# Three blocks of a language model on one core: the first unit of four layers works on x times the norm's weights, and the root comes in behind it

## Chip, core and metric

One core of one Trainium2 chip runs the whole program in one launch. The metric is the device time in microseconds. Every number of the trace is from one profiled execution.

## What is computed

x is 256 x 1024 in float32, and every weight is float32 in HBM (217 MB are read once). Two layers (pooling with spatial gating; gated linear attention with stick-breaking attention), then a block of feed-forward, a mixer (short convolution and an S5 state space), and a second feed-forward. Ahead of each stands the same thing: a norm, a scale and a shift that depend on the condition (columns of `ada`).

```python
def rms_norm(x, gain):
    return x * lax.rsqrt(jnp.mean(x * x, -1, keepdims=True) + EPS) * gain
mod = silu(cond) @ w_mod + b_mod                      # nine vectors of 1024; likewise ada_w for the first two layers
h = rms_norm(x, ffn1_norm) * (1 + sc1) + sh1
x = x + 0.5 * g1 * ((silu(h @ w_gate) * (h @ w_up)) @ w_down)
h = rms_norm(x, mix_norm) * (1 + sc2) + sh2
b_gate, c_gate, v, u = split(h @ w_in)                # 512 columns each
y_conv = b_gate * conv3(c_gate * v)
y_ssm = s5(u); y_ssm = y_ssm * sigmoid(y_ssm @ glu_w + glu_b)
x = x + g2 * (concat(rms_norm(y_conv), rms_norm(y_ssm)) @ w_out)
```

For a column of the weights W, h @ W is r (x G) @ W + sh @ W, with r the reciprocal root of the token, G = gain (1 + scale) per channel, and sh the shift.

## The kernel before

**Form of the data.** x is kept transposed in `xT`, eight tiles of 128 channels x 256 tokens. Each fp32 product is done as three fp32r products: high times high, high times low, low times high. ACT makes a high part by a copy that rounds (`WH` of weights, `hh` of h, `YH` of outputs), DVE makes the low part by a difference (`WL`, `hl`, `YL`).

**Units and pieces.** The weights are cut into units of 1 MB, each of two pieces of 128 x 1024. SP loads them in the order of `unit_list` (L106) into a ring of ten pieces. `cut` on ACT (L1176) makes WH up to three pieces ahead, `cut` on DVE (L1652) WL up to two ahead; four of each are kept, so WL of a piece also waits until PE is through with the piece four back. `cols_T` (L622) is a unit of 256 output columns, output transposed: eight k tiles with 6 products of 256 columns each. `wide` (L634) has hh and hl as the stationary side and 512 weight columns moving, and is used for the FFN's gate and up columns together. `out_rows` (L678) adds 256 rows of the output weights into `pacc`, 48 products; the last of a layer goes by quarters, so that `update` (L1763) on DVE can add each quarter to xT while PE does the next.

**ada.** The scales and shifts come from further units that only DVE works on: each half unit is one multiply and add of 128 x 1024 into `ACC` (L1675), the sums over the partitions are done by PE, and an "add" on DVE (L1681) stores eight columns. `weave` (L125) spreads these units among the others; `ada_places` (L191) says at which unit DVE does them, with a place "tail" behind the last unit of a layer.

**The seam between two layers.** Behind the last `out_rows`: ACT squares the eight tiles of the new xT, PE sums them over the channels (`stats`, L661), DVE computes the root in eight short dependent instructions (`newton`, L1717 to L1726), PE spreads it over the partitions (`spread`, L671), and `modulate` makes for each k tile on DVE xT times GS times root (L1755), on ACT the shift and high part hh, on DVE the low part hl (L1760). The first product of the next layer needs tile 0 of these. `norm_mod` (L731) and, ahead of FFN 1, the lines L1045 to L1051 put products on constants (`warm`) between. At FFN 1 two statistics are taken with weights `FG2`, as the first model's final norm stands in between; half of these sums stand between the quarters of the last out_rows. DVE's columns GS are made behind the update (`mod_cols`, L1740).

**Side work.** Preparation for S5 in FFN 1 and in MIX is written as generators; `side.run` takes `rate` steps of them per piece on each engine. PE's transposes ct (L981, L988) are such steps, with 6 idle ones ahead. PSUM has four banks for units, given in turn by `open_` and `back`. In MIX the order on PE is u, u, c, v, b, c, v, b, with the S5 steps in, out and turn (transposes back, L1098) between, then glu, which needs Y_G0 and Y_G1 (gelu of both halves of the S5 output; `gelu`, L2302), and the conv statistics.

**GpSimd** issues the S5 parameter loads (L2441, L2443) behind the last unit of the odd layer, masks the attention weights (L2402), and does little else.

## Time and profile before

| | us |
|---|---|
| median of 3 runs (lowest, highest) | 985.44 (983.79, 986.64) |
| the profiled execution | 985.16 |
| its span in the trace | 983.4 |
| PE busy | 951.5 |
| DVE busy | 713.7 |
| ACT busy | 508.8 |
| POOL busy | 40.9 |

Times in the rows are from the start of the span. The span is 1.8 us shorter than the execution's own time; what is compared with other runs is the latter. Busy times overlap; a row of a timeline ends with the idle time of its engine just ahead of it and with what ended that.

### The profile page before, as it was taken

What the parts mean: (1) busy time and instruction counts of PE and PEld (TensorE: products, weight loads), DVE (VectorE), ACT (ScalarE), POOL (GpSimd) and SP (SyncE); (2) the same over time, 40 slices, a digit from 0 to 9 for tenths busy, and PEclk for the clock granted to TensorE, in tenths of its full rate; (3) what the DMA queues carried; (4) which work ended last, traced back from release to release, by engine and by line L of the source; (5) the groups of instructions that cost most, each with busy time, mean ns of one, the idle gap of its engine ahead of it and who ended that gap; (6) DMA issues with size and microseconds to landing.
All of it is one profiled execution on the core that took longest, in us unless ns stands there. A gap on an engine that the chain in (4) does not pass through costs nothing.

```text
span 983.4 us, 17238 instructions
## 1 busy us (share of the span) xinstructions
PE 951.5 (97%) x7025; PEld 875.3 (89%) x7025; DVE 713.7 (73%) x994; ACT 508.8 (52%) x745; POOL 40.9 (4%) x68
## 2 busy tenths in 40 slices
PE   6999999999999999999999999999999999999998
PEld 5799989989899889999778889889998978898987
DVE  4778877767957946675998988967888765555554
ACT  4654364446645555644755456475555554444444
POOL 2100000000000013210100000000000000000000
PEclk9999999999999999999999999999999999999999
DMA  9998676846875877576577887774534457676631
GB/s 365 385 342 257 211 268 231 283 129 226 291 259 167 295 261 250 179 260 213 155 254 255 281 274 263 246 257 136 172 119 138 131 172 247 184 223 212 192 101 43
DMA packets 134247, 219.43 MB, mean 223 GB/s; under 512 B 8585, under 2 KB 100090, under 8 KB 134168
## 3 DMA queue, kind: packets, MB, share of 16 engines
q1 hardware_dynamic: 132416, 214.99, 66.3%
q0 software_dynamic: 992, 1.76, 0.7%
q10 hardware_dynamic: 760, 1.59, 0.4%
q8 instruction: 55, 0.90, 0.4%
q14 instruction: 24, 0.20, 0.1%
HBM read 217.25 MB, written 1.05 MB: 222 GB/s over the span
## 4 chain that ended last, share of the span: by engine, by line
PE 88%; DVE 7%; DMA 2%; issue 2%; ACT 1%; ACTq 0%; DVEq 0%
PE pw L568 62%; PE pacc L568 24%; DVE WL L1659 1%; DMA ring<-in_ada_w 1%; DVE SQT L1755 1%; DVE hl L1760 1%; PE pw L1021 1%; DMA cst<-in_consts 1%; DVE ACC L1675 1%; ACT hh L1174 1%; DVE AR L1675 0%; PE pw L997 0%; DVE xT L2059 0%; ACT WH L1174 0%; ACT SQT L1174 0%
## 5 line engine op out<-in xcount | busy, mean ns | idle before, releaser
L1174 ACT ACTIVATE WH<-ring 128x1024 fp32r<-128x1024 f32 x288 | 302.7, 1057 | 271.1 <-PE pw L568 171.7
L1659 DVE TENSOR_TENSOR WL<-ring,WH 128x1024 fp32r<-128x1024 f32 x288 | 348.3, 1224 | 84.2 <-ACT WH L1174 83.5
L568 PE MATMUL pacc<-YH,WH 128*128 128x256 f32 x672 | 192.8, 287 | 2.7 <-issue 1.7
L568 PE MATMUL pacc<-YH,WL 128*128 128x256 f32 x672 | 190.1, 283 | 0.0
L568 PE MATMUL pacc<-YL,WH 128*128 128x256 f32 x672 | 190.0, 283 | 0.0
L568 PE MATMUL pw<-hh,WH 128*128 128x256 f32 x704 | 186.7, 287 | 1.5 <-DVE WL L1659 0.8
L568 PE MATMUL pw<-hh,WL 128*128 128x256 f32 x704 | 183.9, 283 | 0.0
L568 PE MATMUL pw<-WH,hh 128*128 128x512 f32 x448 | 177.3, 396 | 2.8 <-DVE WL L1659 2.3
L568 PE MATMUL pw<-WL,hh 128*128 128x512 f32 x448 | 175.2, 391 | 0.0
L568 PE MATMUL pw<-hl,WH 128*128 128x256 f32 x704 | 142.6, 284 | 0.0
L568 PEld LDWEIGHTS pw<-hh,WH 128*128 128x128 f32 x704 | 134.8, 191 | 6.0 <-issue 5.7
L1174 ACT ACTIVATE AR<-pw 128x512 f32<-128x512 f32 (+8 forms) x180 | 80.3, 467 | 113.8 <-PE pw L568 110.5
L568 PE MATMUL pw<-WH,hl 128*128 128x512 f32 x448 | 138.4, 390 | 0.0
L568 PEld LDWEIGHTS pw<-hh,WL 128*128 128x128 f32 x704 | 135.0, 192 | 0.0
L568 PEld LDWEIGHTS pacc<-YH,WH 128*128 128x128 f32 x672 | 128.7, 192 | 5.4 <-issue 3.0
L568 PEld LDWEIGHTS pacc<-YL,WH 128*128 128x128 f32 x672 | 128.8, 192 | 0.7
L568 PEld LDWEIGHTS pacc<-YH,WL 128*128 128x128 f32 x672 | 128.7, 192 | 0.0
L1675 DVE SCALAR_TENSOR_TENSOR ACC<-ring,PC,ACC 128x1024 f32<-128x1024 f32 x95 | 121.7, 1281 | 2.4 <-DMA ring<-in_ada_w 2.2
L568 PEld LDWEIGHTS pw<-hl,WH 128*128 128x128 f32 x704 | 109.5, 192 | 0.1
L568 PEld LDWEIGHTS pw<-WH,hh 128*128 128x128 f32 x448 | 84.5, 189 | 23.2 <-DVE WL L1659 3.6
L568 PEld LDWEIGHTS pw<-WH,hl 128*128 128x128 f32 x448 | 84.4, 188 | 18.0
L568 PEld LDWEIGHTS pw<-WL,hh 128*128 128x128 f32 x448 | 84.5, 189 | 16.4
(272 smaller groups left out, 778.2 us busy)
## 6 DMA issues: line engine op xcount, KB each, us to landing
ring<-in_w_mod SPq DMA_DIRECT2D x72, 512.0 KB, 4.7
ring<-in_odd_in_w SPq DMA_DIRECT2D x56, 512.0 KB, 5.8
ring<-in_ada_w SPq DMA_DIRECT2D x48, 512.0 KB, 6.9
ring<-in_ffn_w_gate SPq DMA_DIRECT2D x88, 256.0 KB, 3.3
ring<-in_ffn_w_up SPq DMA_DIRECT2D x88, 256.0 KB, 4.3
ring<-in_ffn_w_down SPq DMA_DIRECT2D x44, 512.0 KB, 4.6
ring<-in_even_in_w SPq DMA_DIRECT2D x40, 512.0 KB, 6.5
ring<-in_even_out_w SPq DMA_DIRECT2D x16, 512.0 KB, 5.6
```

What stands on the lines that cost most here:

```text
L568: return eng.matmul(o, a, b, start=start, stop=stop, skip_group_check=True)
L1021: last = eng.transpose(pb[:, n * T + m * P:n * T + m * P + P], fbuf(blk, m)[:, n * P:n * P + P], ident)
L1174: return eng.activation(dst, src, func, **kw)
L1659: tt(WL[:, i % NL, :], slot(half_of(i)), WH[:, i % NH, :].bitcast(F32), SUB).then_inc(s_lo, 1)
L1675: stt(out=acc, in0=slot(g), scalar=wc, in1=acc, op0=MUL, op1=ADD).then_inc(s_ada, 1)
L1755: stt(out=SQT[:, k, :], in0=xT[:, k, :], scalar=GS[:, k:k + 1], in1=rb, op0=MUL, op1=MUL).then_inc(s_u, 1)
L1760: stt(out=hl[:, q, :], in0=SQT[:, q, :], scalar=m[:, q:q + 1], in1=hh[:, q, :].bitcast(F32), op0=ADD, op1=SUB).then_inc(s_hl, 1)
```

## The change

At the seams ahead of the odd layer, FFN 1, MIX and FFN 2 the first unit (qk0, gate and up columns of block 0, c, likewise) no longer waits for the root. ACT makes hh as the high part of xT times GS per tile (`early`), GpSimd makes xT times GS again and its low part hl (`lows`), and PE runs the first unit on these (`first`), with two more columns that hold the shift, so that their result is sh @ W. Half of the statistics come ahead of tile 0, half behind it, the spreading of the root ahead of tile 4. ACT copies both halves of the raw result (`RAW`) and the spread root (`RB`) to SBUF, GpSimd multiplies them (`rooted`), and ACT adds the shift's part (`biased`, or inside the Silu). From the second unit on the modulated tiles are used as before; DVE makes them with WL cuts between. The fillers at the seams go, GS is made ahead of the update, and the ada sums and adds go from the tails and the first two units (`QUIET`) to other units. In both FFNs gate and up columns of block 0 become two units in `cols` form, and the four transposes of that block go. The low-rank gate's 24 products go among the k tiles of qk1 and behind it, one output gate unit of the odd layer goes ahead of `at`. MIX begins with c, and the S5 steps keep their distances to the u units, with one unit fewer ahead of glu. The S5 parameter loads are issued after oo1 instead of oo7.

The diff, cut to its core:

```diff
-    def weave(side, from_, clear=0):
...
         k = 0
         for i, u in enumerate(main):
-            while k < len(side) and (2 * k + 1) * (len(main) - clear) <= 2 * i * len(side):
...
     def ffn(tag, Wg, Wu, Wd):
         for b in range(12):
-            if b < 11:
+            if b == 0:
...
+                cols(f"{tag}u0", Wu, 0)
+            elif b < 11:
...
-    weave(ada(a0, 2, 3) + ada(a1, 0, 2), at, 3)
+    weave(ada(a0, 2, 3) + ada(a1, 0, 2), at, 4)
...
-    weave(ada(a1, 2, 3) + ada(a2, 0, 4), at, 3)
+    weave(ada(a1, 2, 3) + ada(a2, 0, 4), at, 3, 2)
...
-    weave(ada(a2, 4, 8), at, 3)
-    for name, c0 in (("wu0", 1536), ("wu1", 1792), ("wc0", 512), ("wv0", 1024), ("wb0", 0), ("wc1", 768),
+    weave(ada(a2, 4, 8), at, 4, 2)
+    for name, c0 in (("wc0", 512), ("wu0", 1536), ("wu1", 1792), ("wv0", 1024), ("wb0", 0), ("wc1", 768),
                      ("wv1", 1280), ("wb1", 256)):
...
-    weave(ada(a2, 8, 9), at)
+    weave(ada(a2, 8, 9), at, 4, 2)
...
+        elif nm not in quiet:
             unit = nm
             add(nm)
-            if summed and summed[0][1]:
+            if summed and summed[0][1] and behind[nm] not in quiet:
                 total(nm)
...
-            if nm in tails:
-                key = "tail " + nm
-                total(key)
-                add(key)
+    assert not added and not summed
...
+FIRST = [None, "qk0", "f1g0", "wc0", "f2g0"]
+QUIET = ("eo7", "qk0", "qk1", "oo7", "f1g0", "f1u0", "f1d10", "wc0", "wu0", "wo3", "f2g0", "f2u0", "f2d10")
...
                         w = ones[:, 0:64] if weights is None else weights[:, k, :].unsqueeze(2).to_broadcast([P, 2, 32])
                         stats(st["pb"][:, 0:256], w, k, SQ_FIN[L] + k, k == 0, k == 7)
+                def rest():
+                    sums(2)
+                    sums(3)
+                    full[f"fin{L}"] = (s_sqr, sqr_n[0])
...
+                later[L] = rest
...
-                    if weights is not None and q >= 2 and h == 0:
-                        sums(q - 2)
                     if q == 3 and h == 1:
-                        if weights is None:
-                            sums(0)
-                            sums(1)
-                        sums(2)
-                        sums(3)
-                        full[f"fin{L}"] = (s_sqr, sqr_n[0])
+                        sums(0)
+                        sums(1)
+                        if L == L_F2:
+                            rest()
                 return tail
-            def norm_mod(L, z):
-                ada("tail " + TAIL[L - 1])
-                back(f"fin{L - 1}")
-                if L >= L_MIX:
-                    warm(5, f"warm{L}a")
-                spread(f"r{L}", 0, z, (s_u, 8 * L + 8), True)
-                warm(4, f"warm{L}b")
+            later = {}
+            def first(L, z, c=0):
+                name = FIRST[L]
+                k, a = unit(name)
+                names = first_banks(L)
+                bks = [open_(nm, None, True) for nm in names]
+                for half in range(2):
+                    H, Lo = piece(2 * k + half, a)
+                    for kk in range(4):
+                        i = 4 * half + kk
+                        if i == 1:
+                            later[L - 1]()
+                            back(f"fin{L - 1}")
+                        if i == 4:
+                            spread(f"r{L}", c, z, (s_rb, L), True)
+                        p.wait_ge(s_eh, 8 * (L - 1) + i + 1)
+                        for m, pb in enumerate(bks):
+                            mm(pb[:, 0:T + 2], H[:, kk, m * P:m * P + P], hh[:, i, 0:T + 2], i == 0, False)
+                            mm(pb[:, 0:T + 2], Lo[:, kk, m * P:m * P + P], hh[:, i, 0:T + 2], False, False)
+                        p.wait_ge(s_el, 8 * (L - 1) + i + 1)
+                        for m, pb in enumerate(bks):
+                            last = mm(pb[:, 0:T + 2], H[:, kk, m * P:m * P + P], hl[:, i, 0:T + 2], False, i == 7)
+                    last.then_inc(s_use, 1)
+                for nm in names:
+                    full[nm] = used(name)
+                    back(nm)
                 back(f"r{L}")
...
-            norm_mod(L_ODD, 2)
...
-            cols_T(L_ODD, "qk0")
...
-            for k in range(8):
-                last = mm3(pb[0:16, 0:T], (GRH[:, k, :], GRL[:, k, :]), hpair(L_ODD, k), k == 0, k == 7)
+            first(L_ODD, 2)
...
+            def low_rank(k):
+                if k == 0:
+                    open_("gl")
+                    p.wait_ge(s_grl, 1)
+                return mm3(pw[place["gl"]][0:16, 0:T], (GRH[:, k, :], GRL[:, k, :]), hpair(L_ODD, k), k == 0, k == 7)
+            cols_T(L_ODD, "qk1", None, lambda k: low_rank(k - 3) if k > 2 else None)
+            for k in range(4, 8):
+                last = low_rank(k)
...
-            cols_T(L_ODD, "qk1")
+            cols_T(L_ODD, "qk2")
...
+            gates = iter(range(8))
+            cols_T(L_ODD, f"og{next(gates)}")
...
-                yield from idle(6)
+                yield from idle(10)
...
+                    if blk == 0:
+                        cols_T(L, f"{tag}u0")
+                        if L == L_F1:
+                            spread("xnew", 8, 4)
+                            side.rate = 1
...
+            first(L_F1, 4, 10)
...
+            first(L_MIX, 5)
             for j in range(2):
                 cols_T(L_MIX, f"wu{j}", [(s_ura, j + 1), (s_urd, j + 1)])
             s5_in(0)
-            cols_T(L_MIX, "wc0")
+            cols_T(L_MIX, "wv0")
             s5_in(1)
-            cols_T(L_MIX, "wv0")
+            cols_T(L_MIX, "wb0")
             s5_out(0)
-            cols_T(L_MIX, "wb0")
+            cols_T(L_MIX, "wc1")
             s5_turn(0)
-            cols_T(L_MIX, "wc1")
+            cols_T(L_MIX, "wv1")
             s5_out(1)
-            cols_T(L_MIX, "wv1")
+            cols_T(L_MIX, "wb1")
             s5_turn(1)
-            cols_T(L_MIX, "wb1")
...
+            def early(L, sh, c, scale=1.0):
+                s.wait_ge(s_gs, L + 1)
+                s.wait_ge(*gone[f"ada{c}"])
+                s.wait_ge(*used(LAST_H[L]))
+                act(hh[:, :, T:T + 2], shift_cols(sh)).then_inc(s_esh, 1)
+                for q in range(4):
+                    ns = (2 * q, 2 * q + 1)
+                    if q == 3:
+                        squares(L - 1, ns)
+                        cut_on(L - 1)
+                    for n in ns:
+                        s.wait_ge(s_x, X_FIN[L - 1] + n + 1)
+                        act(hh[:, n, 0:T], xT[:, n, :], scale=GS[:, n:n + 1]).then_inc(s_eh, 1)
+                    if q < 3:
+                        squares(L - 1, ns)
+                k = unit(FIRST[L])
+                cut(2 * k)
+                modulate(L, sh, range(4))
+                for m, nm in enumerate(first_banks(L)):
+                    s.wait_ge(*full[nm])
+                    act(RAW[L][:, m, :], pw[place[nm]][:, 0:T + 2], scale=scale).then_inc(s_bank[place[nm]], 1)
+                cut(2 * k + 1)
+                modulate(L, sh, range(4, 8))
+                act(RB[L], pw[place[f"r{L}"]][:, 0:T]).then_inc(s_rb, 1)
+            def biased(L, dsts, func=ACT.Identity):
+                for m, dst in enumerate(dsts):
+                    s.wait_ge(s_em, 2 * (L - 1) + m + 1)
+                    act(dst, dst, func, bias=RAW[L][:, m, T:T + 1]).then_inc(s_eu, 1)
...
+                pieces(f"{tag}u0")
+                if tag == "f1":
+                    evac("xnew", XNW, src=pw[place["xnew"]][:, 0:T])
+                    side.rate = 1
+                for m in range(2):
+                    s.wait_ge(s_em, 2 * (L - 1) + m + 1)
+                    act(fbuf(0, m), fbuf(0, m), ACT.Silu, bias=RAW[L][:, m, T:T + 1]).then_inc(s_sl, 1)
...
+            win("wb1", lambda: s5_rows(1))
+            yhigh(Y_G0, f2(YS[:, 0:2, :]), (s_gelu, 2))
             conv_squares(0)
+            gelu(1, 0)
+            conv_squares(1)
...
+            def between(L, g, sh, root):
+                update(L - 1, g)
+                k = unit(FIRST[L])
+                root()
+                cut(2 * k)
+                mods[0] += 1
+                modulate(L, sh, range(3))
+                cut(2 * k + 1)
+                modulate(L, sh, range(3, 8))
...
+            def lows(L, sh):
+                g.wait_ge(s_esh, L)
+                g.wait_ge(s_gs, L + 1)
+                eng.tensor_tensor(hl[:, :, T:T + 2], shift_cols(sh), hh[:, :, T:T + 2].bitcast(F32), SUB)
+                for k in range(8):
+                    xg = XG[L][:, k % 2, :]
+                    g.wait_ge(s_x, X_FIN[L - 1] + k + 1)
+                    eng.tensor_scalar(xg, xT[:, k, :], GS[:, k:k + 1], None, MUL).then_inc(s_eg, 1)
+                    g.wait_ge(s_eh, 8 * (L - 1) + k + 1)
+                    g.wait_ge(s_eg, 8 * (L - 1) + k + 1)
+                    eng.tensor_tensor(hl[:, k, 0:T], xg, hh[:, k, 0:T].bitcast(F32), SUB).then_inc(s_el, 1)
+            def rooted(L, dsts):
+                g.wait_ge(s_rb, L)
+                for m, nm in enumerate(first_banks(L)):
+                    g.wait_ge(*gone[nm])
+                    eng.tensor_tensor(dsts[m], RAW[L][:, m, 0:T], RB[L], MUL).then_inc(s_em, 1)
```

## Rows read from the trace of the kernel before

**Rows 1.** The page of the kernel before, its part 1
```profile
PE 951.5 (97%) x7025; PEld 875.3 (89%) x7025; DVE 713.7 (73%) x994; ACT 508.8 (52%) x745; POOL 40.9 (4%) x68
```

**Rows 2.** The chain that ended last, in order of time (start us, us, what)
```profile
192.92 17.46 PE pacc L568 x144
...
216.24 59.40 PE pw L568 x408
...
464.56 0.92 PE pacc L568 x6
...
667.14 8.63 PE pacc L568 x72
...
760.71 17.27 PE pacc L568 x144
777.98 2.04 PE pw L568 x64
...
831.11 10.91 PE pw L568 x48
...
861.99 0.44 PE pw L1021 x4
```

**Rows 3.** Timeline of PE at the seams (start, us, instruction, idle before)
```profile
461.48 0.73 PE L568 MATMUL pw<-RS,SQT 128*64 128x64 f32 x12 [0.41 <-ACT SQT L1174]
...
478.38 0.50 PE L568 MATMUL pw<-WH,hh 128*128 128x512 f32 x1 [0.78 <-DVE WL L1659]
...
688.62 0.36 PE L568 MATMUL pw<-hh,WH 128*128 128x256 f32 x1 [0.75 <-DVE WL L1659]
...
790.72 0.50 PE L568 MATMUL pw<-WH,hh 128*128 128x512 f32 x1 [1.26 <-DVE WL L1659]
```

**Rows 4.** Timeline of DVE at the seam into FFN 2
```profile
774.56 1.65 DVE L1769 SCALAR_TENSOR_TENSOR xT<-pacc,MOD,xT 128x256 f32<-128x256 f32 x4
...
781.56 0.16 DVE L1726 SCALAR_TENSOR_TENSOR RS<-RS 128x2 f32<-128x2 f32 x1
...
783.65 0.48 DVE L1760 SCALAR_TENSOR_TENSOR hl<-SQT,MOD,hh 128x256 fp32r<-128x256 f32 x1 [0.18 <-ACT hh L1174]
...
789.45 4.62 DVE L1659 TENSOR_TENSOR WL<-ring,WH 128x1024 fp32r<-128x1024 f32 x4
```

**Rows 5.** Groups of ACT by form: busy us, mean ns of one
```profile
L1174 ACT ACTIVATE SQT<-xT 128x256 f32<-128x256 f32 x40 | 15.8, 416 | 18.4 <-DVE xT L1769 18.4
```

**Rows 6.** Groups of POOL by form: busy us, mean ns of one
```profile
L2402 POOL TENSOR_SCALAR_AFFINE_SELECT AR<-AR 128x512 f32<-128x512 f32 x2 | 1.2, 635 | 36.8 <-ACT AR L1174 36.8
...
L2402 POOL TENSOR_SCALAR_AFFINE_SELECT AR<-AR 128x1024 f32<-128x1024 f32 x1 | 1.1, 1085 | 21.0 <-ACT AR L1174 21.0
```

**Rows 7.** Timelines of DVE and POOL in stick-breaking attention
```profile
371.37 1.30 DVE L1659 TENSOR_TENSOR WL<-ring,WH 128x1024 fp32r<-128x1024 f32 x1
...
382.45 2.44 DVE L1659 TENSOR_TENSOR WL<-ring,WH 128x1024 fp32r<-128x1024 f32 x2
...
382.60 2.44 POOL L2402 TENSOR_SCALAR_AFFINE_SELECT AR<-AR 128x128 f32<-128x128 f32 x2 [1.04 <-DVE AR L2012]
```

**Rows 8.** Timelines of DVE and PE in the pool unit
```profile
133.00 2.67 DVE L1675 SCALAR_TENSOR_TENSOR ACC<-ring,PC,ACC 128x1024 f32<-128x1024 f32 x2
...
136.37 0.36 PE L568 MATMUL pw<-YH,WH 128*128 128x256 f32 x1 [1.77 <-issue]
```

**Rows 9.** Timeline of PE in FFN 1
```profile
507.93 1.12 PE L988 MATMUL pw<-cst,AR 128*128 128x128 f32 x4 [2.31 <-DVE YL L1705]
```

**Rows 10.** Windows: busy us of PE, PEld, DVE, ACT, POOL, granted clock, DMA share, GB/s
```profile
508.00:512.00 4.00, 4.00 (x14) 3.34 (x15) 3.93 (x6) 0.76 (x2) 0.00 (x0) 0.61 0.90 296
```

**Rows 11.** Timelines of PE, ACT and DVE at the end of MIX
```profile
747.80 0.35 PE L568 MATMUL pw<-YH,WH 128*128 128x256 f32 x1 [0.46 <-DVE YL L1705]
...
741.50 1.11 ACT L1174 ACTIVATE AR<-pw 128x256 f32<-128x256 f32 x2
...
746.97 0.68 DVE L1705 TENSOR_TENSOR YL<-AR,YH 128x512 fp32r<-128x512 f32 x1
```

More of the change, by code:

```diff
@@ L129, in weave @@
         for i, u in enumerate(main):
-            while k < len(side) and (2 * k + 1) * (len(main) - clear) <= 2 * i * len(side):
+            while k < len(side) and (2 * k + 1) * (len(main) - clear - lead) <= 2 * (i - lead) * len(side):
                 units.append(side[k])
@@ L218, in ada_places @@
     m, unit = 0, None
+    names = [u[0] for u in units if u[0] != "ada"] + [None]
+    behind = dict(zip(names, names[1:]))
     for nm, *_ in units:
@@ L490, in build @@
         XNW = ar(512 * 3, T)
+        EW = [0, 16384, 8192, 19464, 8192]
+        RB = [ar(o, T) for o in EW]
+        XG = [v3(ar(o + T, 2 * T), 2) for o in EW]
+        RAW = [v3(ar(o + T, 2 * T + 4), 2) for o in EW]
         def fbuf(blk, m):
@@ L630, in cols_T @@
                                     (half == 0 and kk == 0, False), half == 1 and kk == 3)
+                        if behind is not None and (half, kk) != (1, 3):
+                            behind(4 * half + kk)
                     last.then_inc(s_use, 1)
@@ L1038, in ffn @@
                                  finish(L) if blk == 11 else None, (lambda: turn(blk)) if blk < 11 else None)
-            def xnew_back():
-                yield from idle(3)
-                back("xnew")
-                yield
-            ada("tail oo7")
-            back("fin1")
-            warm(6, "warm2a")
-            spread("r2", 10, 4, (s_u, 24), True)
-            spread("xnew", 8, 4, None, True)
-            warm(5, "warm2b")
-            back("r2")
-            side.gens.append(xnew_back())
-            side.rate = 1
+            side.rate = 0
             side.gens.append(s5_weights())
+            first(L_F1, 4, 10)
             ffn(L_F1, "f1", Y_F1)
             side.flush()
-            norm_mod(L_MIX, 5)
             def s5_in(h):
@@ L1358, in _, with gate @@
             eng.preload_act_table_set("silu_and_others")
+            def gate(j):
+                pieces(f"og{j}")
+                evac(f"og{j}", f2(GT[:, 2 * j:2 * j + 2, :]), func=ACT.Silu)
+            gate(0)
             s.wait_ge(s_kqe, 3)
@@ L1515, in ffn @@
                         if blk == 1:
-                            yhigh(y0, pw[place[f"{tag}t0"]][:, :], full[f"{tag}t0"])
+                            yhigh(y0, ar(0, 2 * T), gone[f"{tag}u0"])
                         pieces(f"{tag}u{blk}")
@@ L1915, in _ @@
                 pieces(f"eo{j}")
+            mod_cols(3, M1, "norm_g", 8)
             v.wait_ge(*gone["ada2"])
-            update(L_EVEN, M0[:, 16:24])
-            norm(L_EVEN)
-            ada("tail eo7")
-            mod_cols(3, M1, "norm_g", 8)
-            modulate(L_ODD, M1[:, 0:8])
+            between(L_ODD, M0[:, 16:24], M1[:, 0:8], lambda: norm(L_EVEN))
             def decay():
@@ L1966, in _ @@
             gates = iter(range(8))
+            pieces(f"og{next(gates)}")
             v.wait_ge(s_kqe, 3)
@@ L2002, in _ @@
                     b.then_inc(s_yf, 1)
-                pieces(f"og{next(gates)}")
+                if q == 0:
+                    pieces(f"og{next(gates)}")
             for j in range(4):
@@ L2181, in ffn @@
             def ffn(tag, y0, n0):
-                for blk in range(12):
+                pieces(f"{tag}u0")
+                if tag == "f1":
+                    side.rate = 1
+                b = place[f"{tag}u0"]
+                for m in range(2):
+                    v.wait_ge(*full[f"{tag}u0"])
+                    v.wait_ge(s_sl, n0 + m + 1)
+                    a = tt(fbuf(0, m), fbuf(0, m), pw[b][:, m * T:m * T + T], MUL)
+                a.then_inc(s_bank[b], 1)
+                for blk in range(1, 12):
                     if blk < 11:
@@ L2199, in half_gate @@
                 v.wait_ge(*v.step(ts(HG, m, 0.5, None, MUL)))
-            side.rate = 1
+            side.rate = 0
             side.gens += [update_x(), s5_coefs(), s5_weights(), s5_tables(), s5_kernel(), s5_skip()]
             ffn("f1", Y_F1, 0)
+            side.flush()
             half_gate(8, M2[:, 16:24])
-            update(L_F1, HG)
-            side.flush()
             mod_cols(9, M2[:, 24:48], "mix_norm")
-            norm(L_F1)
-            ada("tail f1d10")
-            modulate(L_MIX, M2[:, 24:32])
+            between(L_MIX, HG, M2[:, 24:32], lambda: norm(L_F1))
             def conv(j):
```

200 lines of the change are left out of this document (98 added, 102 removed).

## Prediction

> **What bounds the kernel now.** I read the page first: PE is busy 97% of 983.4 us, DVE 73%, ACT 52%, POOL 4% [rows 1]. So only PE time counts: what it has to do, and where it waits. The chain in order of time gives PE's own pace: 144 products of 256 columns in 17.27 us (0.12 each), 48 of 512 columns in 10.91 (0.227 each), the 64 of the norm's statistics in 2.04, four transposes in 0.44 [rows 2]. At that pace a unit of 48 x 256 takes 5.76 us. Then PE's timeline shows where it stands still. There are four seams, where one layer's output ends and the next layer needs its norm. Call E the end of the last product into pacc: 210.38, 465.48, 675.77 and 777.98 [rows 2]. At FFN 2 DVE has the root at 781.72 and makes the first hl at 783.65, E + 5.7 [rows 4]; of the time to there 2.04 are statistics, and the fillers behind them are no work. The second unit waits again, 1.26 us, for a low part of weights (WL) [rows 3], because DVE makes all the modulated tiles first and the WLs only from 789.45 [rows 4]. I take the start of the third unit as the yardstick: 790.72 + 5.46 = E + 18.2 here, 688.62 + 5.76 = E + 18.6 at MIX, 478.38 + 5.46 = E + 18.4 at FFN 1 [rows 3], and at the odd layer 216.24 + 6.3 + 2.9 + 5.8 (DVE-paced qk0, low-rank gate, qk1) = E + 20.9 [rows 2].
>
> **The seam after the change, without port trouble (FFN 2, times from E).** DVE updates x at the same times plus 0.2 for the columns now made ahead of it. ACT now does 16 instructions of 0.416 us [rows 5] there instead of 8 (a product with GS and a square per tile), so the last square is done at 2.9 instead of 1.6, the statistics at 3.3 instead of 2.0, the root at 5.0 instead of 3.7. PE does tile 0 ahead of the second half of the statistics, tiles 1 to 3 while the root is computed, spread (0.45), tiles 4 to 7: each tile is 6 products, 0.72, and the unit ends at 8.8. DVE goes on from the root with one WL (1.15 each by the four in 4.62 us [rows 4]), three modulated tiles (two instructions each, 0.8: there are 14 from 783.65 to 789.45 [rows 4]), the next WL at 9.2 to 10.3, five tiles. ACT puts the two RAW copies and a WH cut between its fourth and fifth hh, so the last hl is at 16.2, not 15. The second unit so ends at 16.6 instead of 14.5, and the third waits for its WL until 17.4. **Gain 0.8**, and 0.44 more because block 0 is born transposed; the narrow products (96 x 0.12 instead of 48 x 0.227, 0.6 dearer) are in the 17.4. So the seam's hole is filled, but DVE, already the pacer, takes most of it back. The same working gives 17.6 at MIX (gain 1.0), 19.0 at the odd layer with the low-rank products filling the waits (gain 1.9). FFN 1 loses today a wait of 0.41 in the tail, twice [rows 3], and 1.0 of statistics stand ahead of E there, which puts its comparable E 1.9 earlier: 18.4 + 1.9 - 17.9 = 2.4, and 0.44. Sum of the seams: -7.0. The two extra columns cost 1 in 128 of 5.76, under 0.05 per seam. The longer table load at the odd layer falls into ACT's wait ahead of the tail.
>
> **GpSimd.** It gets eight pairs per seam, a product (one input) and a difference (two inputs), then two products with the root. Its only comparable rows are masks: 0.635 us for 512 elements, 1.085 for 1024 [rows 6], so 0.88 ns per element and 0.185 fixed; 256 elements with one input 0.41, with two between 0.41 (the second input free) and 0.64 (twice the reading), taken near the upper end. A pair is then some 1.15 us, the eighth is ready at E + 6.6, PE wants it at 8.6: covered, up to 1.4 us a pair. At 2.0 a pair each seam would lose about 4.5.
> The Trainium skill (GPSIMD Engine Reference, 3.1) states 2.6 cycles per element for two inputs; as an estimate from that page the difference would take 0.7 us and the sum stays as it is.
>
> **The port.** While POOL masks 128 elements next to DVE's WLs, each mask takes as long as a WL (2.44 for two, beside two WLs in 2.44) instead of the 0.3 that the two rows above give for 128 elements, and the WLs are stretched by under 0.1 (1.30 for one [rows 7]; four undisturbed in 4.62 [rows 4]): the two engines exclude each other where DVE reads two SBUF tiles, and DVE loses about what POOL reads. In the seam the root is eight dependent instructions 0.2 us apart, seven of them with two SBUF inputs, exactly while POOL works on pairs. Bounds: 0 (they are a few elements wide and slip between), and 7 x 0.5 = 3.5 us (each meets a two-input read of the length worked out above). I take 1.3, two or three meetings, nearer to the lower bound because the fixed part of POOL's instructions leaves gaps as long as a root step. It lies on the chain root, spread, modulate, third unit; with the hl's it costs 1.6 per seam: **+6.3**.
> The Trainium skill (SBUF — State Buffer, "SBUF: two separate sides") says the shared pair is an exclusive lock held for the whole instruction. By that rule the upper bound is nearer; it is the slower rival below.
>
> **Two stalls elsewhere.** In the pool unit PE waits 1.77 us while DVE does two ada halves, 2.67 us from 133.00, ahead of the YL that PE needs [rows 8]. With the new weave (12 side units over 25 instead of 26 positions) that side unit falls to eg7, whose DVE time has a hole: **-1.7**. In FFN 1 the transposes ct0 wait 2.31 us for a bank that DVE's YL frees [rows 9], and behind that wait the granted clock is 0.61 of full speed over four us, most of them at the 1.2 GHz level [rows 10]: another 1.6. After the change ct0 comes ten pieces behind u0, at the output product of block 1, where the next bank in turn is that of a gate long read: **-3.9**. If the bank order is otherwise, 0.
>
> **End of MIX.** c comes first, so u and the whole S5 chain are one unit later while glu stays where it is. Today turn(1) is followed by wb1 (5.76 us of cover), and still glu waits 0.46 [rows 11]. After the change turn(1) stands directly ahead of glu. Behind turn(1), ACT has wb1's copy, the high part of G0 and two squares (six times 256 elements, 2.5 by [rows 5], some 1.9 since two of them are 512 wide), then the yt copies; from these to the low part of G1 it takes 741.50 to 747.65, 6.15 [rows 11]; minus the WL inside (1.15), plus conv gate and conv squares that now stand ahead of tanh (1.3 to 1.9), about 6.7. PE has glu's first half (24 x 0.12) and the conv statistics (half of 2.04), 3.9. 1.9 + 6.7 - 3.9 - 0.46 less the turn itself, about 0.44: **+3.8**. If the clock falls behind this wait as it fell behind ct0's, up to 1.6 more; something above the middle, **+1.0**. Biased sits ahead of a WH cut on ACT, and waits for POOL; behind the third unit's start that shows as +0.3 at MIX. The S5 side work of FFN 1 ends two units later, beside the YL for the last output: +0.3. In SP's queue only the order of loads changes; POOL's four DMA issues move out of the seam and are hidden by 30 us of idle POOL.
>
> **Sum** against the profiled execution (985.16, its span 983.4 and 1.76 around it; 0.28 under the median of 985.44): -7.0 + 6.3 - 1.7 - 3.9 + 3.8 + 1.0 + 0.6 = -0.9, so 984.3, and 984.5 against the median.
>
> **Rivals.**
> - Port free (chance 0.25): root steps slip through, the 6.3 of the above goes: 978.2. For: they move two to four elements. Against: [rows 7].
> - Port decides (0.18), the slower one: every root step meets POOL, the root is 2.6 to 3.5 us late, 3.2 at the third unit, so +12.8 instead of +6.3: 991.0. It is slower than before once a seam loses over 2.6. For: DVE's stretched WL. Against: only the reading excludes.
> - ct0 or another bank wait stays in FFN 1 (0.12): DVE is near full there, and its side work is packed closer: +4, 988.4.
> - The change doesn't do what it says (0.05): POOL over 1.6 us a pair, PE waits for POOL's low parts instead of the root: at 2.0 a pair 4 x 4.5 in place of the 6.3, 996.
> - My forecast (0.40): 984.5.
>
> About 0.3%, 3 us, is what a measurement of this kernel tells from no change. Faster: 0.25 and a third of my case, 0.38. Slower: 0.18 + 0.05, half of the ct0 case, little of mine: 0.30. Same 0.32. Range 977 to 991, over the first two rivals; outside remain POOL too slow and the far ends.
>
> **What would show it.** Right: the fillers are gone, PE's wait for the root under 2 us per seam, third units at E + 17.5 to 19.5, root steps stretched where POOL reads, no wait at ct0 and in the pool unit, and a new wait ahead of glu of 3 to 5 us. Root steps 0.2 apart would put me in the fast rival; PE waiting for hl of POOL in the last one. No new wait at glu would make the end of MIX wrong, and the whole 4.8 us with it.

## The result, and the profile after

The changed kernel takes 1006.05 us (median of four runs, 1005.63 to 1007.47), the kernel before, beside it, 985.5: ratio 1.0213, 95% interval 1.0194 to 1.0231. It is 20.5 us slower; 984.5 was forecast, with a range of 977 to 991. Medians, here and below, leave out single executions in a slow state (1161 us and more). The profiled execution has a span of 1003.6, 20.2 more than the 983.4 of before. Part 1 of its page, beside [rows 1]:

```profile
PE 957.4 (95%) x7047; PEld 876.9 (87%) x7047; DVE 723.4 (72%) x994; ACT 523.7 (52%) x795; POOL 112.9 (11%) x144
```

Where the 20.2 lie is found by the marks of the prediction. E, the end of the last product into pacc, is now at 207.4, 468.1, 684.9 and 793.5. Against 210.4, 465.5, 675.8 and 778.0 [rows 2] the even layer is 3.0 shorter, then each stretch from E to E is longer: +5.6, +6.4, +6.4, and +4.7 from the last E to the end. So every stretch with a seam pays. PE's view of waits says for what (engine and tile <- whom it waited for: us in total, times, longest):

```profile
PE pw L586 <- POOL hl L2505: 14.1, 15, 1.8
...
PE pw L586 <- DVE ACC L1748: 3.3, 2, 2.5
PE pw L586 <- DVE YL L1778: 2.7, 2, 1.7
PE pw L586 <- DVE RS L1799: 2.0, 4, 0.7
PE pw L586 <- DVE AR L2276: 1.9, 1, 1.9
```

Of these the kernel before had the root (3.6 there) and YL (0.5, and 2.3 at ct0). The largest is the last rival of the prediction, chance 0.05: PE waits for GpSimd's low parts. POOL's timeline in the seam into FFN 2 (start, us, line and operation, idle before):

```profile
790.81 0.93 POOL L2502 TENSOR_SCALAR AR<-xT,PC 128x256 f32<-128x256 f32 x1
791.89 0.74 POOL L2505 TENSOR_TENSOR hl<-AR,hh 128x256 fp32r<-128x256 f32 x1
792.61 0.93 POOL L2502 TENSOR_SCALAR AR<-xT,PC 128x256 f32<-128x256 f32 x1
...
799.05 1.80 POOL L2505 TENSOR_TENSOR hl<-AR,hh 128x256 fp32r<-128x256 f32 x1
800.83 0.92 POOL L2502 TENSOR_SCALAR AR<-xT,PC 128x256 f32<-128x256 f32 x1
...
803.84 1.40 POOL L2505 TENSOR_TENSOR hl<-AR,hh 128x256 fp32r<-128x256 f32 x1
```

A pair starts every 1.80 us (790.81, 792.61), where 1.15 was forecast: the product takes 0.93, not 0.41, the difference 0.74, near the 0.64. And two differences are far longer, 1.80 and 1.40. DVE's timeline there shows why:

```profile
797.36 0.66 DVE L1794 TENSOR_TENSOR RS<-RS 128x2 f32<-128x2 f32 x1
798.05 0.41 DVE L1795 SCALAR_TENSOR_TENSOR RS<-RS 128x2 f32<-128x2 f32 x1
...
799.04 1.22 DVE L1732 TENSOR_TENSOR WL<-ring,WH 128x1024 fp32r<-128x1024 f32 x1
```

At 799.04 DVE starts a WL; POOL's difference starts at 799.05 and ends 0.59 behind the WL's end: it stood still meanwhile. The other way round, two root steps of two elements take 0.66 and 0.41 instead of 0.16. The first ends at 798.02, with POOL's difference (797.25 to 798.00):

```profile
797.25 0.75 POOL L2505 TENSOR_TENSOR hl<-AR,hh 128x256 fp32r<-128x256 f32 x1
797.97 0.93 POOL L2502 TENSOR_SCALAR AR<-xT,PC 128x256 f32<-128x256 f32 x1
```

The Trainium skill (SBUF — State Buffer, "SBUF: two separate sides") has this as a lock that is held for the whole instruction and that the second to come waits for; by the WL and by this step the trace agrees. The second step doesn't fit so well: it ends at 798.46, in the middle of POOL's product (797.97 to 798.90), and the steps behind it take 0.15 to 0.16 while that product still runs. But it turned out otherwise than in the prediction: DVE lost 0.75 at the root (1.25 at MIX, where three steps are stretched), and POOL, already late, lost 1.7 (1.80 and 1.40 for 0.74). PE's timeline, up to the third unit:

```profile
799.27 0.68 PE L586 MATMUL pw<-cst,RS 128*128 128x128 f32 x4 [0.36 <-DVE RS L1799]
800.90 0.51 PE L586 MATMUL pw<-hl,WH 128*128 128x258 f32 x2 [0.47 <-POOL hl L2505]
802.67 0.51 PE L586 MATMUL pw<-hl,WH 128*128 128x258 f32 x2 [0.78 <-POOL hl L2505]
805.30 0.62 PE L586 MATMUL pw<-hl,WH 128*128 128x258 f32 x2 [1.63 <-POOL hl L2505]
...
814.50 0.47 PE L586 MATMUL pw<-WH,hh 128*128 128x512 f32 x1 [0.45 <-DVE WL L1732]
```

The waits have a second price: behind them the granted clock falls to the 1.2 GHz level, for 3 to 7 us. The windows 694 to 706 and 801 to 813 (busy us of PE, PEld, DVE, ACT and POOL, granted clock, DMA share, GB/s):

```profile
694.00:706.00 12.00, 9.24 (x57) 8.74 (x57) 9.20 (x16) 5.22 (x11) 6.22 (x6) 0.72 0.20 64
...
801.00:813.00 12.00, 9.29 (x61) 8.58 (x62) 8.01 (x17) 5.88 (x13) 6.07 (x7) 0.86 0.29 87
```

The first unit ends at E + 14.1 to 14.6 (8.8 forecast), third units start at E + 23.9, 25.7, 21.8 and 21.1 instead of the 20.6, 19.5, 19.2 and 19.0 that the working gives with its 1.6 for the port. Outside the seams PE's timeline has three more places:

```profile
269.69 1.08 PE L586 MATMUL pw<-ACC,cst 128*32 128x256 f32 x8 [2.53 <-DVE ACC L1748]
...
493.23 0.64 PE L586 MATMUL pw<-ACC,cst 128*32 128x256 f32 x8 [1.93 <-DVE AR L2276]
...
756.56 0.36 PE L586 MATMUL pw<-YH,WH 128*128 128x256 f32 x1 [1.68 <-DVE YL L1778]
```

The first two are sums of the conditioning that stand one unit behind DVE's last half, or want the bank that u0 still holds; the third is the forecast wait ahead of glu.

And one thing that the change does without meaning to: it stretches the rows of hh and hl from 256 to 272 elements. In the chain, 48 products of 512 columns now take 11.13 (before 10.91, [rows 2]).

### The profile page after: what moved, and what is told of

It reads as the page before. It is cut to its first block, busy times and chain, and to the rows that moved or that the text cites. A ratio compares the mean times of both kernels' runs of the same rounds, so it can differ in the third digit from the quotient of the medians.

```text
span 1003.6 us, 17449 instructions
## 1 busy us (share of the span) xinstructions
PE 957.4 (95%) x7047; PEld 876.9 (87%) x7047; DVE 723.4 (72%) x994; ACT 523.7 (52%) x795; POOL 112.9 (11%) x144
## 4 chain that ended last, share of the span: by engine, by line
PE 78%; DVE 7%; POOL 6%; issue 3%; ACT 3%; DMA 2%; SPq 0%; DVEq 0%; POOLq 0%; ACTq 0%
PE pw L586 55%; PE pacc L586 21%; POOL AR L2502 3%; POOL hl L2505 3%; DMA ring<-in_ada_w 2%; DVE WL L1732 2%; DVE ACC L1748 1%; ACT AR L1214 1%; PE pw L1071 1%; ACT WH L1214 1%; DVE AR L1748 0%; PE pw L1047 0%; ACT hh L1214 0%; DVE AR L1965 0%; DVE AR L1972 0%
## 5 line engine op out<-in xcount | busy, mean ns | idle before, releaser
L586 PE MATMUL pw<-hh,WH 128*128 128x256 f32 (+1 forms) x768 | 206.2, 290 | 0.2 <-DVE WL L1732 0.2
L586 PE MATMUL pw<-hh,WL 128*128 128x256 f32 (+1 forms) x768 | 201.8, 284 | 0.0
L586 PE MATMUL pacc<-YH,WL 128*128 128x256 f32 x672 | 190.1, 283 | 0.0
L586 PE MATMUL pacc<-YL,WH 128*128 128x256 f32 x672 | 190.1, 283 | 0.0
L586 PE MATMUL pw<-hl,WH 128*128 128x256 f32 (+1 forms) x768 | 157.4, 287 | 14.1 <-POOL hl L2505 14.1
L586 PE MATMUL pw<-WH,hh 128*128 128x512 f32 x416 | 166.3, 400 | 1.3 <-DVE WL L1732 1.2
L586 PE MATMUL pw<-WL,hh 128*128 128x512 f32 x416 | 163.5, 393 | 0.0
L586 PEld LDWEIGHTS pw<-hh,WH 128*128 128x128 f32 x768 | 148.7, 194 | 5.2 <-issue 4.3
L586 PEld LDWEIGHTS pw<-hh,WL 128*128 128x128 f32 x768 | 148.7, 194 | 0.1
L1214 ACT ACTIVATE AR<-pw 128x512 f32<-128x512 f32 (+9 forms) x186 | 81.9, 461 | 117.4 <-PE pw L586 116.2
L586 PEld LDWEIGHTS pw<-hl,WH 128*128 128x128 f32 x768 | 120.6, 194 | 17.4 <-POOL hl L2505 17.4
L586 PE MATMUL pw<-WH,hl 128*128 128x512 f32 x416 | 129.6, 393 | 0.0
```

Source lines behind the costliest of these rows:

```text
L586: return eng.matmul(o, a, b, start=start, stop=stop, skip_group_check=True)
L1214: return eng.activation(dst, src, func, **kw)
```

## The experiments

Four theories. **1**: GpSimd's low parts are too slow, and this is most of the loss. **2**: the fall of the clock behind the waits is a large part of it. **3**: the row stride of hh changes the pace of PE's products. **4**: the new places of the side units make the waits at 269 and 493. The rival to 1 is the prediction's own picture: DVE paces the seam, so moving work to DVE costs what it saves. "The kernel with the low parts on DVE" is the changed kernel with this edit:

```
-  eng.tensor_scalar(xg, xT[:, k, :], GS[:, k:k + 1], None, MUL)       (GpSimd)
-  eng.tensor_tensor(hl[:, k, 0:T], xg, hh[:, k, 0:T].bitcast(F32), SUB)
+  stt(out=hl[:, k, 0:T], in0=xT[:, k, :], scalar=GS[:, k:k + 1],        (DVE, in update)
+      in1=hh[:, k, 0:T].bitcast(F32), op0=MUL, op1=SUB)
```

> The changed kernel with the eight low parts of each first unit made by DVE in one instruction each ((x times GS) minus hh, 0.4 us) between its updates of x, instead of a product and a difference on GpSimd (0.93 + 0.74 us, a pair every 1.79). If GpSimd's pace is what costs (theory 1): PE's 14.1 us of waits for hl are gone, and so is the half clock behind them (5.5 us of products at 0.213 instead of 0.12 in each seam); the first unit ends at E + 9 instead of E + 14.3 (11.8 at the pace of DVE, if the last low parts delay the root); third units near E + 18; 12 to 17 us less than the changed kernel: 989 to 994. If instead DVE was the pacer of the seam anyway, as the prediction had it (rival): the low parts on DVE push its root and its WLs back by the 3.3 us that they take, waits for WL appear in place of those for hl, and it stays within 5 us of 1006.

Measured 991.79 (990.73 to 995.0), ratio 1.0071 (1.0047 to 1.0095): 14.3 us less than the changed kernel. PE's waits now:

```profile
PE pw L586 <- ACT hh L1215: 4.7, 8, 1.0
PE pw L586 <- DVE WL L1733: 3.5, 6, 1.3
PE pw L586 <- DVE RS L1800: 3.4, 4, 1.3
PE pw L586 <- DVE ACC L1749: 3.3, 2, 2.5
PE pw L586 <- DVE AR L2289: 3.2, 1, 3.2
```

The 14.1 for hl are gone, the clock is 1.00 in each seam of this profile, and the root steps take 0.16 again. Theory 1 holds. The third unit starts at E + 18.7 in FFN 2, though, and at 18.2 before: this seam is back at what it was, no better, and the first unit ends 1.0 later than the forecast 8.8. DVE's timeline shows the step that is missing in the working:

```profile
784.82 0.88 DVE L1854 SCALAR_TENSOR_TENSOR hl<-xT,PC,hh 128x256 fp32r<-128x256 f32 x2 [1.34 <-ACT hh L1215]
785.61 0.15 DVE L1783 TENSOR_SCALAR RS<-pw 128x2 f32<-128x2 f32 x1
```

DVE waits for the last two high parts, which on ACT stand behind a WH. **The root ahead of these two low parts:**

```
   root()
+  low(L, 6); low(L, 7)
   cut(2 * k)
```

> The kernel with the low parts on DVE, and the last two of them behind the root instead of ahead of it. There DVE waits 1.34 us for ACT (a WH stands ahead of the last two high parts) and starts the root at E + 4.6, though the statistics are done at E + 3.3. If the root sets the end of the first unit and that the high parts of the modulated tiles 4 to 7 (which overwrite it): spread, first unit's end and third unit 1.0 us earlier in each of four seams, 991.8 - 4 = 988. If DVE's sum of work sets the third unit: unchanged within 1 us, 991 to 992.

990.56 (988.77 to 992.82), ratio 1.0057 (1.0039 to 1.0075). The first unit does end at E + 8.7, but the third starts at 18.2 (802.0 - 783.8) instead of 18.7: half of the gain is taken up by the wait for ACT's hh and for WL. The four third units are 0.5, 0.3, 0.2 and 0.5 earlier, and the medians stand 1.2 apart, with ranges that overlap. The forecast 4 is 1 to 2: DVE and ACT pace the seam, as the prediction had it.

**The clock alone.** Fillers ahead of the late low parts of the changed kernel, first 4, 7, 13 and 7 of them, then half:

```
+  if i >= 4:
+      warm((4, 7, 13, 7)[i - 4], f"warm{L}{i}")      second run: (2, 3, 7, 3)
   p.wait_ge(s_el, 8 * (L - 1) + i + 1)
```

> The changed kernel with 31 filler products (128 columns) in each seam, 4, 7, 13 and 7 of them ahead of the four low parts that PE waits for, so that PE is never idle there. The wait itself stays. If the granted clock's fall behind the waits has a price of its own (theory 2): second units run at 0.12 a product instead of 0.213, some 2.4 us less per seam, 8 to 10 us in all, 996 to 998. If DVE sets the time of the third unit anyway: under 2 us less, 1004 to 1006.

1012.34 (1010.8 to 1013.77), a miss: a filler takes 0.21 us, so 31 of them lasted longer than the waits.

> The changed kernel with 2, 3, 7 and 3 fillers (each takes 0.21 us by the first such run: the 31 there lasted 6.6 us per seam against 3.7 us of waits, so it was overfilled by 2.9) ahead of the four late low parts: 3.2 us of fillers in waits of 3.7, nothing delayed by them. If the fall of the granted clock behind the waits has a price (theory 2): second units at 0.12 instead of 0.213 a product, the third unit 1 to 2.4 us earlier per seam, 996 to 1002. If the low parts of the modulated tiles and the WLs set the third unit anyway: 1005 to 1007, with a longer wait for WL instead of the slow products.

1002.33 (1001.71 to 1004.67), ratio 1.0185 (1.0161 to 1.0210); and the granted clock from 797.3 to 809.3, the same part of the last seam, is 1.00. That is 3.7 us less than the changed kernel, but not 0.9 in each seam. From E to E the two profiles differ by 3.0, 0.3, 0.3 and 0.2 us. Of the 3.0 only 1.5 are in the seam (third unit at E + 22.4 instead of 23.9); the rest comes behind the wait at 269, where the granted clock fell in the changed kernel's profile and did not in this one, in code that is the same. In the seam into FFN 1 a fall is left, half as long as before. So the fall in the seams is worth some 2.3 us by these profiles, less than the 2.4 per seam that was expected: in FFN 2 the third unit waits 1.0 for a WL instead. Theory 2 holds for a tenth of the loss, and is part of theory 1's 14.3.

**The stride alone**, on the kernel before:

```
-  hh = sb("hh", [P, 8, T], F32R)          hl likewise; GRW and RR move into other buffers to make room
+  hh = sb("hh", [P, 8, T + 16], F32R)[:, :, 0:T]
```

> The kernel before with nothing changed but the row stride of hh and hl, 272 instead of 256 elements (and the arena rearranged to make room). In the changed kernel products of 512 columns with hh as weights take 232.0 ns instead of 227.2, and those of 256 columns with hh as moving data 117.1 instead of 120.0. If the stride does that (theory 3): the same two paces here, 1344 x 4.8 = +6.5 us and 2112 x -2.9 = -6.1 us, so 985 to 987 in sum, FFN layers 2.3 us longer each, the others shorter. If the paces come from something else of the change: 227 and 120 as before, 985.5.

986.01 (985.71 to 987.82), ratio 1.0007 (0.9997 to 1.0018), and both paces as in the changed kernel. From the chains in order of time, 48 wide and 48 narrow products, first the kernel before:

```profile
737.44 5.96 PE pw L568 x48
...
814.02 10.91 PE pw L568 x48
```

and with the stride of 272:

```profile
735.94 5.84 PE pw L569 x48
...
830.05 11.13 PE pw L569 x48
```

Theory 3 holds: wide products, with hh as weights, 227 to 232 ns; narrow ones, with hh moving, 120 to 117 from start to start. The two cancel, which is why nothing of it was seen in the sum. They need not: **two strides**, 256 in the FFNs (whose products are wide), 272 elsewhere. In the code it is the other way round with the names, `narrow` is the view with rows of 256:

```
+            flat = t.rearrange("p a n -> p (a n)")
+            wide_, narrow = t[:, :, 0:T], flat[:, 0:8 * T].rearrange("p (a n) -> p a n", a=8)
+            return [wide_, wide_, narrow, wide_, narrow]      (even, odd, FFN 1, MIX, FFN 2)
```

> The kernel before with a stride of 272 elements for hh and hl in the even, the odd and the MIX layer, and of 256 in both FFNs. If the stride sets the pace (theory 3): 227 ns for the 960 wide products of the FFNs and 117 for the narrow ones of the other layers: -6.1 for the narrow, +1.8 for 384 wide ones that keep the 272: 981 to 982. If not: 985.5.

982.57 (981.82 to 983.49), ratio 0.9972 (0.9962 to 0.9982): faster than the kernel before by 0.3%, with the change left out altogether. On the kernel with the low parts on DVE:

> The kernel with the low parts on DVE, and the modulated tiles of both FFNs at a stride of 256 elements (the early ones and the other layers keep 272). By theory 3, which the first runs bear out: 960 wide products x 4.8 ns = 4.6 us less, 987.2. If the stride matters only together with the order of the kernel before: 991.8.

989.37 (987.97 to 991.2), ratio 1.0046 (1.0030 to 1.0061): 2.4 less instead of 4.6. In its profile the products of FFN 2, from E to their end, take 196.3 instead of 198.7: 2.4 less, as the theory has it for one FFN. From the first E to that of MIX it is 1.1 longer, though, instead of 2.3 shorter; the next run shows from what.

**MIX as before** (u first, no early unit, its fillers), on the kernel with the low parts on DVE:

```
-  first(L_MIX, 5)                          and c first
+  later[L_F1](); back("fin2"); warm(5, "warm3a")
+  spread("r3", 0, 5, (s_u, 8 * L_MIX + 8), True); warm(4, "warm3b"); back("r3")
```

> The kernel with the low parts on DVE, and MIX as in the kernel before: no early unit there, order u0, u1, c0, v0, b0, c1, v1, b1, its seam with fillers; odd layer and both FFNs as changed. The prediction had the end of MIX at +4.8 and its seam at -1.0 (port apart). By the traces MIX takes 105.8 us from E to E here against 102.2 before, so, with 1.2 us of faster narrow products, undoing it should give 3.6 to 4.8: 987 to 988. If the wait ahead of glu came from DVE's or ACT's load and not from the order: 991 to 992, and the wait for the low part of G1 stays 1.7 us.

989.71 (987.9 to 990.75), ratio 1.0049 (1.0032 to 1.0066), 2.1 less. By its profile MIX takes 101.4 from E to E instead of 105.8, the 4.4 expected, and the wait ahead of glu is back at 0.5. But the stretch ahead of it, from the first E to that of MIX, is 4.1 longer, in code that is the same but for the end of FFN 1. The window 262 to 276, first with the low parts on DVE, then this kernel:

```profile
262.00:276.00 14.00, 11.50 (x101) 10.27 (x100) 9.67 (x12) 7.34 (x11) 1.02 (x2) 1.00 0.96 324
```

```profile
262.00:276.00 14.00, 11.50 (x86) 10.26 (x85) 9.88 (x12) 6.29 (x9) 0.45 (x1) 0.88 0.98 324
```

The same 2.5 us wait at 265, and behind it the clock falls in one execution and not in the other (the profile with the two strides has 0.88 too). At 360 the two stand 1.6 apart. The other 2.6 come in the same way at the seam into FFN 1, at the same wait of 3.2 us ahead of g1, in the window 478 to 492:

```profile
478.00:492.00 14.00, 10.85 (x63) 8.79 (x62) 13.67 (x21) 10.24 (x15) 2.35 (x2) 1.00 0.51 152
```

```profile
478.00:492.00 14.00, 10.33 (x51) 8.21 (x52) 12.89 (x20) 7.33 (x13) 2.35 (x2) 0.76 0.42 126
```

So the profile of the kernel with the low parts on DVE is one of its lucky executions (990.7, the highest took 995.0), and the medians of these kernels, of four to seven executions each, carry such falls of the clock, 1.5 us and more apiece, in differing numbers.

**The side units placed otherwise**, so that each sum stands two units behind its last half:

```
-  weave(ada(a1, 2, 3) + ada(a2, 0, 4), at, 3, 2)       weave(ada(a2, 4, 8), at, 4, 2)
+  weave(ada(a1, 2, 3) + ada(a2, 0, 4), at, 2, 1)       weave(ada(a2, 4, 8), at, 4, 4)
+  QUIET: "f1g1" added
```

> The kernel with the low parts on DVE, and the side units placed otherwise: odd layer weave(..., 2, 1) instead of (3, 2), FFN 1 (4, 4) instead of (4, 2) with f1g1 among the quiet units, so that every sum of the conditioning stands two units behind its last half and none stands right ahead of g1. By the traces the sum of part 5 waits 2.5 us at 265 for DVE's ACC, and the sum ahead of g1 of FFN 1 3.2 us for the bank that u0's product frees. If the placing of the side units is what put these waits there: both gone, 991.8 - 5 = 986 to 988. If DVE is simply late there, whatever the place (rival): the waits turn up at the next product of those banks, and the time stays within 1.5 us of 991.8.

985.39 (984.94 to 986.67), ratio 0.9998 (0.9988 to 1.0008): 6.4 less, and equal to the kernel before. Both waits are gone, and the clock does not fall once in this profile; theory 4 holds. Low parts and side units, 14.3 + 6.4, make up the 20.5. On the changed kernel itself:

> The changed kernel, low parts on GpSimd as in the change, with only the other placing of the side units (odd layer 2, 1; FFN 1 4, 4, g1 quiet). With the low parts on DVE this placing gave 6.4 us (991.8 to 985.4). If the two costs stand side by side: 1006.1 - 6.4 = 999 to 1001, the wait of 2.5 at the sum of part 5 and that of 1.9 ahead of g1 gone. If GpSimd's late products of block 0 hold the bank there anyway: a wait at g1 or u1 stays and only 3 are gained, 1003.

997.07 (996.86 to 999.09), ratio 1.0121 (1.0104 to 1.0138): 9.0 less, 2.6 more than on the other one. Taken in this order the split is 9.0 for the side units and 11.7 for the low parts. Part of the 2.6 may be the clock, which fell behind the wait at 269 in the changed kernel's profile and not in the other's; it was not separated.

**The pool unit.** The kernel before with two strides and, in the even layer alone, weave's clear 4 for 3:

> The kernel before with the two strides (982.6), and the side units of the even layer alone placed as in the change (weave's clear 4 for 3). The prediction had the wait of 1.77 us in the pool unit gone by it, -1.7. If so 980.8 with no wait at 136; if that wait comes from the pool unit's own chain: 982.6.

980.10 (979.36 to 980.65), ratio 0.9944 (0.9929 to 0.9959), 2.5 less than with the strides alone; the wait at 136 is gone, and with it a fall of the clock that stood behind it in the profile with the strides alone.

**All of the mending together:**

> All of the mending together: low parts on DVE, the last two behind the root, a stride of 256 for the FFNs' modulated tiles, side units as in the run with the other placing, MIX as in the kernel before. If the terms add up: 991.8 - 2.3 - 1.2 - 2.1 - 5 = 981 by the medians of the single runs; the early unit in three seams would then be worth 2 us less than nothing against the kernel before with the two strides (982.6). If the terms share one slack (DVE's queue): 984 to 987.

974.13 (973.85 to 975.23), ratio 0.9889 (0.9872 to 0.9907): 11 us faster than the kernel before, 32 faster than the changed one. It is better than the 981 that the single runs sum to. The waits at 265 and 483 are not in it, behind which the clock fell in some of their executions, and the granted clock is 0.999 over the span; that this is the whole difference is argued, not shown. Of the change it keeps the early unit in three seams; its PE waits:

```profile
PE pw L593 <- ACT hh L1228: 5.6, 7, 1.1
PE pw L593 <- DVE WL L1746: 3.1, 5, 1.2
```

What the early unit brings differs by seam. FFN 2 starts its third unit at E + 18.2, as before. The odd layer does at E + 19.1 (20.9 by the prediction's working for the kernel before), FFN 1 at 18.5 (20.3 before, with the 1.9 that the prediction adds because half of the statistics stood ahead of E): 1.8 each. The strides bring 3.2 and the pool unit 2.5 by their own runs. Beside the profile of the pool unit's run, which has both, the stretches from E to E are 249.7 for 254.6 in the odd layer, 208.6 for 208.8 in FFN 1 and 101.4 for 101.4 in MIX, and 204.9 for 205.4 from the last E to the end. The wait at ct0 is gone, but FFN 1 from its third unit to its E takes 190.1 in both: 1.7 for a YL of the last output and 0.6 ahead of another step stand in its place, and in the profile of the pool unit's run the clock had not fallen behind ct0.

**Rows of 264 for YH and YL too**, on the kernel before with two strides and on the mended one:

> The kernel before with two strides, hh and hl at 264 elements outside the FFNs, and YH and YL at 264 too, instead of 256. The 2016 products into pacc take 119.9 ns in every kernel so far; hh as moving data went from 120.0 to 117.1 at a stride of 272. If any row stride that is no multiple of 256 elements makes a moving operand faster: 2016 x 2.8 = 5.6 us less than 982.6, 977. If it is the 272 that counts, or only hh's place: 982 to 983 with narrow hh products back at 120 and wide ones at 227 in the layers without 256, about 983.

980.96 (980.17 to 981.97), ratio 0.9956 (0.9939 to 0.9972), 1.6 less than with the two strides alone. The 144 products into pacc of the chain take 17.00 instead of 17.27 [rows 2], 118.1 ns each instead of 119.9, so part of the expected effect; the narrow products with hh, at 264 instead of 272, go from 117.1 to 117.8.

```profile
757.11 17.00 PE pacc L575 x144
```

> The mended kernel (974.1) with rows of 264 elements for hh, hl, YH and YL: products into pacc go from 119.8 to 118.1 (2016 x -1.7 = -3.4 us), narrow hh products of the even, odd and MIX layers from 117.1 to 118.3 (2112 x +1.2 = +2.5). By the stride theory 973 to 974; if the fewer columns of padding cost nothing: 970.5. Slower than 975 would speak against the stride as the cause.

974.07 (972.77 to 974.23), ratio 0.9880 (0.9862 to 0.9897): equal to the mended kernel. By the paces 2016 x 1.8 ns less and 2112 x 0.7 ns more would leave 2 us; in this profile the clock falls once, at the end of FFN 1 (0.57 from 660 to 664), and FFN 1 is 1.1 longer. More was not separated.

## Why the prediction was wrong

**The step that failed is the price of GpSimd's pair.** The prediction put it at 1.15 us, from masks of 512 and 1024 elements [rows 6], and covered up to 1.4. It is 1.80, and 2.9 beside a WL (797.97 to 800.83). The difference was nearly right (0.74 for 0.64); the product was not: 0.93 for 0.41. A mask has no scalar per partition, and a line through two masks says nothing about an instruction that has one. The last rival had the right form: it gave 996 and 4.5 per seam at 2.0 a pair, and the third units are 2.1 to 3.3 later than forecast in three seams and 6.2 in FFN 1, of which 4.4 go with the other placing of the side units. It got a chance of 0.05, though [rows 7] had a price beyond the cover: a mask beside a WL takes 1.22 us, a pair at that price 2.4, far beyond the 1.4 from which POOL decides. That row was read for what DVE loses and not for what POOL loses.

**The seam without the port** was worked out about right. With the low parts on DVE the first unit ends at 9.7 (8.8 plus the 1.3 of DVE's wait for ACT, minus some slack), third units at 19.6, 19.2, 18.5 and 18.7 once the placing is mended, for 19.0, 17.9, 17.6 and 17.4. Of the missing 1.0 some 0.4 is the wait for the last two high parts, by the run that moves them behind the root; the rest was not assigned. That DVE takes back much of what the early unit gains is right: against the 20.9, 20.3, 18.6 and 18.2 of before the seams gain 1.3, 1.1 and 0.1, and the last loses 0.5.

**The port** was taken at 1.3 in the root; two steps were stretched, 0.75. It was right in kind and too dear in place (the MIX seam, with three steps and 1.25, came near); POOL lost more than DVE (1.06 and 0.66 in two differences), which the prediction did not count, since it had POOL covered. The "port decides" rival (991.0) is out: of seven steps two are stretched, three at MIX.

**Stalls elsewhere.** The pool unit's wait vanished: -1.7 forecast, 2.5 by the run made for it. The wait at ct0 and the slow clock behind it vanished, -3.9 forecast; but the slow clock was there in some executions of the kernel before only, and in the mended kernel other waits in FFN 1 take the place of ct0's. **What was not seen** is that the same new placing brings sums to one unit behind their halves and to u0's bank: 2.5 and 1.9 us in the changed kernel (3.2 with the low parts on DVE), with the clock on top where it falls, 6.4 in all. The prediction followed the side units where there was a stall to lose, and not where one could arise. It is the second step that failed.

**End of MIX.** Forecast +3.8 ahead of glu, +1.0 for the clock. The wait is 1.68, then 1.06 at glu's second half, the first half runs slow (4.5 us for 24 products; the clock falls at 757.7): undoing MIX gives 4.4 in its own stretch, with the seam. Sum right, parts not. The +0.3 for a late YL at the end of FFN 1 is 1.6.

**Paces.** That hh's rows change the time of PE's products was not in the sum at all. It came out at nothing only because two effects of 6 us cancel.

Put together: the low parts on GpSimd cost 14.3, where the sum had 6.3 for the port; the side units cost 6.4, where it had nothing. What is left of the change was forecast at -7.2 and measures 0 (985.4 against 985.5): four seams 1.0 later make 4, the YL at the end of FFN 1 1.3; the last 2 were not assigned. A single fall of the clock, which one execution has and the next has not, is nearly as large.

## What to carry to other kernels

Before work is moved to an engine that has hardly any rows, ask for each operation what in it no row shows (a scalar per partition, a second input), let the price range at least to double, and see whether the cover ends inside that range: if so, that rival is no outsider. When a list of side units is respaced, write down for every sum and bank how far it now stands behind what it waits for, not only where an old stall was. And when a change slows a kernel, undo its parts one by one, and compare several executions of each: here the two faults hid parts that were worth having (of the 11 us in the end 3 are the strides and 8 the change's own, without its MIX), and a price read off one pair of profiles took in falls of the clock that came by chance.

## What the runs showed of the hardware

- GpSimd: 256 elements times a scalar per partition 0.93 us, a difference of two tiles 0.74, one every 1.80 with the gaps. The second agrees with the Trainium skill (GPSIMD Engine Reference, 3.1), whose 2.6 cycles per element for two inputs gave 0.7 as an estimate; that the one-input product is the dearer of the two was not to be expected.
- The row stride of a tile that PE reads changes the pace of its products. hh at 256, 264 and 272 elements: narrow products (hh moving) 119.9, 117.8, 117.1 ns; at 272 the wide ones (hh as weights) 231.9 instead of 227.3. YH and YL at 264: 118.1 instead of 119.9. Why is open; no run here varied the start of a tile alone.
- GpSimd and DVE, beside each other: a root step with two SBUF inputs that meets a GpSimd difference ends with it (0.63 to 0.68 instead of 0.16, in all four seams); one that meets a GpSimd product of 0.93 us is held only until the product is 0.5 us old (0.41), and later steps take 0.16 beside the same product. The starts and ends of GpSimd's instructions in a profile are rough.
- Behind one and the same wait of 2.5 us at 265 to 269, in code that is the same there, the granted clock over the 14 us window from 262 was 1.00 in two profiled executions (low parts on DVE; the second run with fillers) and 0.88 in five. The kernel before shows the same in its times: its executions fall into groups near 983.8, 985.3 and 986.7 us at a mean granted clock of 1.000, 0.998 and 0.996. A price for a fall of the clock is a price with a chance.
